# Router of a mixture-of-experts block: gathered rows made already turned, router tiles in groups of two, one and one, a fifth weight slot filled early, table work around the first SiLU product

## The reference

```
h = rmsnorm(x, ffn_norm)
g_logits = h @ w_group                       # 8 groups
g_sel = argmax(g_logits);  g_w = softmax(g_logits)[g_sel]
e_logits = (h @ w_expert)[group g_sel]       # 8 experts of a group
top_p, top_i = top_k(softmax(e_logits), 2)
gates = g_w * top_p / sum(top_p)
for each of the 2 choices e of a token:
    y += gate * ((silu(h @ w1[e]) * (h @ w3[e])) @ w2[e])
out = rmsnorm(x + y)
```

## Time and profile before

| | before |
|---|---|
| median of 3 runs | 1443.67 us (1443.07 to 1448.06) |
| profiled execution, device time | 1446.29 us |
| its span of instructions | 1444.5 us |
| PE busy | 1389.5 us, 96% |
| DVE busy | 528.9 us, 37% |
| ACT busy | 515.6 us, 36% |
| POOL busy | 473.9 us, 33% |
| read from HBM | 289.27 MB, 202 GB/s over the span |
| chain that ended last, by engine | PE 23%, DMA 13%, DVE 1% |

### The profile page before, as it was taken

One profiled execution on the slowest core, in us unless ns is written; L12 is line 12 of the kernel. 1 busy time (PEld: TensorE's weight loads), 2 busy tenths in 40 slices (PEclk: granted clock), 3 DMA queues, 4 the chain that ended last, 5 costly groups with the idle time before them and its releaser, 6 DMA issues. The chain is left out here.

```text
span 1444.5 us, 26677 instructions
## 1 busy us (share of the span) xinstructions
PE 1389.5 (96%) x11124; PEld 1041.7 (72%) x11124; DVE 528.9 (37%) x1262; ACT 515.6 (36%) x1084; POOL 473.9 (33%) x457
## 2 busy tenths in 40 slices
PE   8999999999999999999999999999999999988986
PEld 7788876677888888888767886876666665655553
DVE  3103217742221200221245404264554554454435
ACT  5325448863332222222346333232223222222222
POOL 5334646543544444444356844410000000000000
PEclk9999999999999999999999999999999999999998
DMA  5223225314133034131232311669999999999994
GB/s 188 83 94 117 97 82 159 105 36 140 59 117 117 30 109 150 62 117 68 82 117 73 117 59 59 241 266 378 411 419 419 420 418 419 421 419 420 420 419 195
DMA packets 89577, 293.22 MB, mean 203 GB/s; under 512 B 9324, under 2 KB 38160, under 8 KB 64880
## 3 DMA queue, kind: packets, MB, share of 16 engines
q1 hardware_dynamic: 89056, 290.35, 52.1%
q0 software_dynamic: 288, 1.05, 0.2%
q10 hardware_dynamic: 112, 0.09, 0.0%
HBM read 289.27 MB, written 2.13 MB: 202 GB/s over the span
## 5 line engine op out<-in xcount | busy, mean ns | idle before, releaser
L504 POOL TENSOR_TENSOR wring_halves<-wring,wring_halves 128x512 fp32r<-128x512 f32 x274 | 357.1, 1308 | 374.4 <-ACT wring_halves L499 372.8
L499 ACT CAST wring_halves<-wring 128x512 fp32r<-128x512 f32 x274 | 168.8, 621 | 450.4 <-PE ps L1239 426.7
L1237 PE MATMUL ps<-wring_halves,big_halves 128*128 128x512 f32 x612 | 241.9, 395 | 0.6 <-POOL wring_halves L504 0.5
L1237 PE MATMUL ps<-hT_halves,wring_halves 128*128 128x512 f32 x480 | 188.2, 392 | 2.4 <-DVE big_halves L2026 2.4
L1239 PE MATMUL ps<-hT_halves,wring_halves 128*128 128x512 f32 x480 | 187.5, 391 | 0.0
L1238 PE MATMUL ps<-big_halves,wring_halves 128*128 128x512 f32 x480 | 187.3, 390 | 0.0
L2721 POOL TENSOR_TENSOR rstd<-rstd,half 128x1 f32<-128x1 f32 (+1 forms) x21 | 12.1, 581 | 506.5 <-DVE rstd L2674 477.7
L1238 PE MATMUL ps<-wring_halves,hT_halves 128*128 128x512 f32 x436 | 170.9, 392 | 0.0
L1239 PE MATMUL ps<-wring_halves,hT_halves 128*128 128x512 f32 x436 | 170.7, 392 | 0.0
L1237 PEld LDWEIGHTS ps<-wring_halves,big_halves 128*128 128x128 f32 x612 | 115.7, 189 | 27.8 <-POOL wring_halves L504 2.7
L1788 PE MATMUL ps<-xn,fixed 128*128 128x512 f32 x256 | 120.0, 612 | 0.4 <-DVE fixed L2469 0.4
(11 more groups left out here) (354 smaller groups left out, 1984.3 us busy)
## 6 DMA issues: line engine op xcount, KB each, us to landing
big<-in_moe_w_dram SPq DMA_DIRECT2D x90, 1024.0 KB, 25.4
wring<-in_moe_w_dram SPq DMA_DIRECT2D x70, 1024.0 KB, 25.2
wring<-in_ffn_w_in_dram SPq DMA_DIRECT2D x22, 1024.0 KB, 7.2
hT<-in_moe_w_dram SPq DMA_DIRECT2D x20, 1024.0 KB, 25.8
wring<-in_fox_w_in_dram SPq DMA_DIRECT2D x7, 2048.0 KB, 8.7
wring<-in_gla_w_in_dram SPq DMA_DIRECT2D x6, 2048.0 KB, 8.4
mkv<-in_moe_w_dram SPq DMA_DIRECT2D x12, 1024.0 KB, 25.8
wring<-in_ffn_w_out_dram SPq DMA_DIRECT2D x4, 2048.0 KB, 7.9
```

Of the source, the lines that this page charges most:

```text
L499: act.copy(hi, src).then_inc(s_hi, 1)
L504: pool.tensor_tensor(lo, src, hi, ALU.subtract).then_inc(s_lo, 1)
L1237: pe.matmul(out, lhs[1], rhs[0], start=start, stop=False)
```

## The change

It has four parts.

- **Turned rows made directly.** For bunch 0, `turned_tokens(t, i)` takes the place of `tokens`, `tokens_out` and `xT`. The rows of `xn` are the stationary operand (128 columns with stride 8) and M is the moving one (128 columns), so the result is `xeT` as it is wanted: 32 products of 128x128 in two banks. The other bunches stay as they were; `s_G` and `s_Ge` count one bunch less.
- **Fifth down slot early.** `rtw` moves to the buffer `fixed`, `down_in(4, 4)` stands behind expert 1's pieces, and SP's wait for `s_lg` goes.
- **Table work around the first SiLU product.** Bunch 0's `placesT` goes behind expert 0's gate/up; six small operations (`spilled_places`) behind `hid(0)`, bunch 1's choices behind `hT_out(0)`, and the gates' arithmetic ahead of `hid(0)`.
- **Router in groups of two, one and one.** `picks`, `ranks` and `choices` take a list of tiles: (0, 1), (2), (3). The counts of all tokens get a bank of their own (`LOGIT_BANKS[2]`). `moe_row(3)` moves from ahead of tile 2's picks to behind its choices, and ScalarE copies the counts only after the last choice (`s_M`).

The core of the diff (SP, ACT, PE, DVE; index changes inside `picks` and `ranks` left out):

```diff
-        rtw = mkv[:, 0:KD * NR].rearrange("p (k n) -> p k n", k=KD)
+        rtw = fixed[:, 912:912 + KD * NR].rearrange("p (k n) -> p k n", k=KD)
...
                 down_in(e, e)
+            down_in(4, 4)
             sp.wait_ge(*tile_release["gwo0"])
...
             gate_up_in(5, 5)
-            sp.wait_ge(s_lg, T)
-            down_in(4, 4)
...
-            act.wait_ge(s_pre, 2)
-            act.copy(cnt, bank(LOGIT_BANKS[1])[:, 2 * EXPERTS:3 * EXPERTS]).then_inc(s_cntc, 1)
+            act.wait_ge(s_M, T)
+            act.copy(cnt, bank(LOGIT_BANKS[2])[:, EXPERTS:2 * EXPERTS]).then_inc(s_cntc, 1)
...
-            tokens_out(0, 0)
-            tokens_out(0, 1)
-            placesT_out(0, 0, 6)
-            xT_out(0, 0, 5)
-            xT_out(0, 1, 7)
+            xT_out(0, 0, 0)
+            xT_out(0, 1, 1)
...
                 silu(b, b)
+                if b == 0:
+                    placesT_out(0, 0, 6)
...
-            added_up(1, [(ones, again(0, 3), 0), (ones, again(1, 3), 0)])
+            added_up(1, [(ones, ohs[:, 0:1, :], 0), (ones, ohs[:, 1:2, :], 0)], True, False)
...
+            def turned_tokens(t, i):
+
+                pe.wait_ge(s_M, t + 1)
+                pe.wait_ge(s_hnrow, t + 1)
+                rows = xn[:, t, :].rearrange("p (m k) -> p k m", k=KD)
+                for k in range(4):
+                    last = pe.matmul(bank(i)[:, k * R:(k + 1) * R], rows[:, 4 * i + k, :], one_hots(0)[1][:, t, :],
+                                     start=(t == 0 and k == 0), stop=(t == T - 1), skip_group_check=True)
+                if t == T - 1:
+                    last.then_inc(s_xTp, 1)
...
-            pe.wait_ge(s_hnrow, T)
-            tokens(0, 0, range(0, 2))
             pe.wait_ge(s_oh, 2)
-            added_up(1, [(ones, again(2, 2), 1), (strict, ohs[:, 2:4, :], 0), (ones, ohs[:, 3:4, :], 2)]).then_inc(s_pre, 1)
-            tokens(0, 1, range(0, 2))
-            tokens(0, 0, range(2, 4))
-            tokens(0, 1, range(2, 4))
-            placesT(0, 6)
-            pe.wait_ge(s_cntc, 1)
-            xT(0, 0, 5)
-            xT(0, 1, 7)
+            added_up(1, [(strict, ohs[:, 2:3, :], 0)], False, True).then_inc(s_pre, 1)
+            added_up(2, [(ones, again(0, 2), 0), (ones, again(1, 2), 0), (ones, again(2, 2), 0)], True, False)
+            turned_tokens(0, 0)
+            turned_tokens(1, 0)
+            pe.wait_ge(s_oh, 3)
+            added_up(2, [(strict, ohs[:, 3:4, :], 0), (ones, ohs[:, 3:4, :], 1)], False, True).then_inc(s_pre, 1)
+            turned_tokens(0, 1)
+            turned_tokens(1, 1)
+            for t in (2, 3):
+                turned_tokens(t, 0)
+                turned_tokens(t, 1)
...
                 expert_in(b)
+                if b == 0:
+                    pe.wait_ge(s_cntc, 1)
+                    placesT(0, 6)
...
-            for p in range(2):
-                picks(p)
-                if p == 0:
-                    output_added(1, T - 1)
-                ranks(p)
-                if p == 0:
-                    moe_scale(T - 1)
-                choices(0, val, range(2 * p, 2 * p + 2))
-                if p == 0:
-                    dve.wait_ge(s_pw, roots.n)
-                    moe_row(T - 1)
+            picks((0, 1))
+            output_added(1, T - 1)
+            ranks((0, 1), 0, 1)
+            moe_scale(T - 1)
+            choices(0, val, (0, 1))
+            picks((2,))
+            dve.wait_ge(s_pw, ROOTS_AHEAD_OF_ROUTER)
+            picks((3,))
...
+            ranks((2,), 1, 2)
+            choices(0, val, (2,))
+            moe_row(T - 1)
+            ranks((3,), 2, 3)
+            choices(0, val, (3,))
...
                     hT_out(b, b)
+                    if b == 0:
+                        bunch_choices(1)
```

More of the change, by code:

```diff
@@ L532, in program @@
         LOGIT_BANKS = SUM_BANKS[1]
+        ROOTS_AHEAD_OF_ROUTER = 1 + 6 * T
         def row_part(v, t, i):
@@ L1757, in _, with added_up @@
             out_projection(first_pair)
-            def added_up(p, parts):
+            def added_up(p, parts, start, stop):
                 for i, (m, v, at) in enumerate(parts):
@@ L1763, in added_up @@
                     last = pe.matmul(bank(LOGIT_BANKS[p])[:, at * EXPERTS:(at + n) * EXPERTS].rearrange("p (t n) -> p t n", t=n), m[:, :], v,
-                                     start=(i == 0 and at == 0), stop=(i == len(parts) - 1), skip_group_check=True)
+                                     start=(start and i == 0), stop=(stop and i == len(parts) - 1), skip_group_check=True)
                 return last
@@ L2418, in _, with picks @@
             dve.wait_ge(s_cst, 2)
[L2420 to L2424, removed]
+            def picks(tiles):
+                a, n = tiles[0], len(tiles)
+                ts = slice(a, a + n)
+                for t in tiles:
                     dve.wait_ge(s_lg, t + 1)
@@ L2427, in picks @@
                 me.wait()
-                for t in (2 * p, 2 * p + 1):
+                for t in tiles:
                     me.inc(dve.max(gm8[:, t, :], lg[:, t, 0:GROUPS]))
                 me.wait()
-                for t in (2 * p, 2 * p + 1):
+                for t in tiles:
                     me.inc(dve.max_index(gi_u[:, t * 8:t * 8 + 8], gm8[:, t, :], lg[:, t, 0:GROUPS]))
@@ L2444, in picks @@
                 picked = ei_u[:, :].rearrange("p (t n) -> p n t", t=T)[:, 0:2, ts]
[L2445 to L2461, removed]
+                chosen = of_tiles(ohall, tiles)
@@ new lines, in picks, with of_tiles @@
+                me.link(dve.tensor_tensor(chosen, ioe.unsqueeze(1).unsqueeze(1).to_broadcast([P, 2, n, EXPERTS]),
+                                          picked.unsqueeze(3).to_broadcast([P, 2, n, EXPERTS]), ALU.is_equal))
+                dve.tensor_tensor(ohs[:, ts, :], chosen[:, 0, :, :], chosen[:, 1, :, :], ALU.add).then_inc(s_oh, 1)
+                me.inc(dve.tensor_copy(of_tiles(esel, tiles), picked))
+            def of_tiles(v, tiles):
+                p, i = divmod(tiles[0], 2)
+                four = v[:, 4 * p:4 * p + 4]
+                four = four.rearrange("p (k t) n -> p k t n", k=2) if len(v.shape) == 3 else four.rearrange("p (k t) -> p k t", k=2)
+                return four[:, :, i:i + len(tiles)]
@@ new lines, in ranks @@
+            def ranks(tiles, b, prefixes):
+                n = len(tiles)
+                r, q, w = of_tiles(rk, tiles), of_tiles(q1, tiles), of_tiles(val, tiles)
+                before = bank(LOGIT_BANKS[b])[:, 0:n * EXPERTS].rearrange("p (t n) -> p t n", t=n)
+                dve.wait_ge(s_pre, prefixes)
+                me.link(dve.tensor_tensor(of_tiles(ohp, tiles), of_tiles(ohall, tiles),
+                                          before.unsqueeze(1).to_broadcast([P, 2, n, EXPERTS]), ALU.mult))
+                me.link(dve.tensor_reduce(r, of_tiles(ohp, tiles), AX, ALU.add))
+                me.inc(dve.tensor_scalar(q, r, C - 0.5, 2.0 * C * EXPERTS, ALU.is_ge, ALU.mult))
+                me.link(dve.scalar_tensor_tensor(out=w, in0=of_tiles(esel, tiles), scalar=float(C), in1=r, op0=ALU.mult, op1=ALU.add))
+                me.link(dve.tensor_tensor(w, w, q, ALU.add))
@@ L2620, in _ @@
                         bunch_places(b - 1)
+                    if b == 0:
+                        spilled_places()
                     hT_out(b, b)
+                    if b == 0:
+                        bunch_choices(1)
                     if b == 3:
```

31 lines of the change are left out of this document (15 added, 16 removed).

## The result

| | before | changed |
|---|---|---|
| median of 22 runs each | 1443.91 us | 1447.76 us |
| lowest to highest | 1440.68 to 1448.36 | 1445.9 to 1452.12 |
| profiled execution, around its span | 1446.29 around 1444.5 | 1448.02 around 1446.2 |

The ratio is 1.0027, with a 95% interval of 1.002 to 1.0034: about 3.9 us slower, where 3.9 us faster was forecast and 1437.9 to 1443.9 given as the range.

The account below looks back on a forecast made before the run. The kernel was taken to end with the experts' weight stream plus a fixed tail. Expert 0's gate/up 3.9 us earlier and later holes 3.8 earlier gave -3.8 to -3.9, so 1439.8 us against 1443.67; range 1437.9 to 1443.9.

Parts of the forecast that it names:

- the price of one record of the new product: TensorE's 64 new gather records: 0.125 us each, taken from the prefix sums, between floor 0.109 and ceiling 0.147.
- the stride shows no price: TensorE's new stationary operand: reading with a stride of 8 elements was claimed to cost nothing extra.
- rows 6: Profile rows of G's strided loads in the turning passes: 128 loads, median 193 ns against a least of 185.
- ceiling of 0.147: Upper bound in us for one record of TensorE's new product, from six prefix-sum records in 0.88 us.
- slower rival: TensorE's 128-column stationary loads not hidden beside products: 0.213 us a record, time +1.5, 1445.2 us; chance 0.05.
- VectorE's chain: VectorE's router tables in the new order: last choice at 968.7 us, 0.8 later than before; gates done at 973.0.
- the clock rival: TensorE's clock falls again during tile 3 and expert 0: gain only 2.2, time 1441.4 us; chance 0.09.
- the second hole of the stream: Weight stream's shortfall in 1005 to 1020 us: 1.9 us missing before, still 1.5 to 2 expected around 1001 to 1016.
- the early slot alone: Fifth down piece sent early into the idle stretch before 940: nothing booked by itself, bounds 0 and 1.5 us.
- VectorE's ceiling: Rival: one tile costs VectorE as much as two, last choice at 971.9; gain 0.8, 1442.9 us; chance 0.10.
- TensorE's floor: Rival: 0.109 us a record and VectorE's half prices, gate/up ends 971.6; gain 5.2, 1438.5 us; chance 0.12.
- nothing arrives: Rival: last weight pieces held by slots, not the stream, so the time stays at 1443.7 us; chance 0.06.

Follow-up runs that it names:

- e2: Changed kernel with normalized rows written by k, VectorE writing with a step of 128 elements, so stationary blocks are contiguous: 1444.28 us, ratio 0.9996.
- e1: Changed kernel with bunch 0's products reading 128 neighbouring columns instead of every eighth (wrong columns, times only): 1440.34 us, ratio 0.9968.
- e10: Changed kernel with rows laid out by twos: VectorE writes in four instructions, TensorE reads with stride 2; whole result computed: 1441.01 us, ratio 0.9972.
- e7: Changed kernel with rows laid out by fours: VectorE in two instructions reading runs of four, TensorE reading with stride 4: 1447.14 us, ratio 1.0022.
- e9: Changed kernel with every fourth column of a stretch of 512 as stationary block (wrong columns): 1447.54 us in one execution.
- e5: Kernel before with only the router's weights in the other buffer and the fifth down piece sent early: 1444.61 us, ratio 1.0005.
- e13: e4 with the table work as before too, leaving the early slot and the router groups: 1443.03 us, ratio 0.9985.
- e12: e10 with the fifth down piece sent late as before, after all logits: 1443.68 us, ratio 0.9991.
- e8: Changed kernel with every second column of a stretch of 256 as stationary block (wrong columns): 1439.81 us in one execution.
- e11: e10 with tile 3's rows scaled by ScalarE and multiplied by the gains on GpSimd instead of VectorE: 1442.49 us, ratio 0.9982.
- e6: Changed kernel with rows kept by k, VectorE reading with a step of 8 and writing contiguously: 1444.03 us, ratio 1.0001.
- e4: Changed kernel with bunch 0 gathered as before (gather, copy, eight turning passes), the rest of the change kept: 1441.94 us, ratio 0.9983.

## Why the prediction was wrong

**The failed step** is the price of one record of the new product: "nearest by shape are the prefix sums ... so 0.125", with the sentence "the stride shows no price". Measured: 0.2375 to 0.242. 64 x 0.115 is 7.4 us; the forecast of -3.9 with 7.4 added is +3.5. In the frame of before, the products start at 962.26 (forecast 962.0) and end at 978.09 (forecast 970.75). In the frame of before the pair goes out at 977.41 + 2.77 = 980.2, 3.4 later than 976.79, and down 3's issue 3.55 later than 1005.51. Everything behind that step worked as described, with the sign turned.

**How rows 6 misled.** They compare turning passes with turning passes, all of them strided, by their own least value. The fair partner stood in the same trace, the turning of M, which is contiguous: 140 ns against 193 (lines 1812 and 1806 above; line 1803 of the kernel before has the same median of 140). In e2, where G is contiguous as well, line 1806 has a median of 140. So the stride cost 53 ns already, under work that hid it: eight turning passes in 1.13 us are 0.14 each. Nor would 53 have been the right surcharge, since the load of a product pays 144 (192 to 336). The unmeasured thing was the load of an FP32 product with a stride of 8, and its ceiling of 0.147 came from contiguous operands alone. A ceiling should have taken the strided load as one that no product hides.

**The slower rival had the right sign and the wrong mechanism.** It put a record at 0.213 and the time at 1445.2. (It calls 0.107 the spacing of the logits; the earlier trace rows give 0.109, so two of them are 0.219.) It decides "from 0.19 us a record on", and the records went past that. But loads of this shape do lie beside the products, 0.111 a record in e1; it is the strided load that can't be hidden. The rule cited there from the Trainium skill, "TensorE: Matmul & The Clock Gate", Part 3, is not borne out by e1. Another page speaks for the step between stride 2 and 4: the Trainium skill, "SBUF — State Buffer", says in "Specifications (TRN2)" that a 16-byte line of SBUF needs at least two hits for full bandwidth. A stride of 2 gives two FP32 elements a line, a stride of 4 one, and 196 and 330 ns agree. The turning passes don't: their loads have a median of 209 ns at a stride of 2 (line 1806 in e10) and 193 at 8. A note under "Door 1: The DMA port swizzle" on that page puts the free stride at 4 FP32 elements; here e7 and e9 contradict it, and the measurement decides.

**Right:** VectorE's chain (last choice forecast for 968.7, measured 966.07 + 2.77 = 968.8); the clock, 1.00 through 966 to 969, so that the clock rival falls; the end of the kernel following the first pair's issue; the second hole of the stream, 2.1 us for a forecast 1.5 to 2; the early slot alone at nothing (e5); the moved table work almost without effect (e13). VectorE's ceiling and TensorE's floor did not come up, and "nothing arrives" is refuted by e1, e7 and e10, which move the end both ways with the chain. The forecast from tile 3's logits to the end of expert 0's gate/up, 959.13 to 972.9, is 13.8 us; e1, with contiguous loads, has 13.84 to the issue behind it. Only half right was that the early slot is worth nothing: e12 says so no longer when the chain is faster. e10, whose records take 0.118 each, comes to the forecast gain, but that is partly luck: by the traces its pair goes out 3.3 us earlier behind the logits (14.32 for 17.66) and down 3's issue 3.1 (43.24 for 46.38), its dearer row scaling costs 0.4 ahead of the logits (14.39 for 13.96 from the first row scaling to tile 3's logits), and the slot that was booked at nothing makes up for it at least in part.

## What to carry to other kernels

Price a new operand by rows of the same mode and the same access pattern; where the trace has none, compare strided with contiguous rows of another mode to see whether a stride costs at all, and take the unhidden price as a bound. A layout that suits TensorE is paid for by the engine that writes it: look for one in which both find two neighbours, as pairs here. A part that is worth nothing beside a slow chain should be tried again once the chain is fast.

## What the runs showed of the hardware

- An FP32 weight load of 128x128 for a product takes 192 ns at stride 1 (e1), 196 at 2 (e8, e10), 330 at 4 (e7, e9) and 336 at 8 (the changed kernel). A record takes 0.111, 0.118, 0.233 and 0.24 us with them. The loads lie over each other, since each is longer than the spacing.
- A load for a turning pass has a median of 140 ns contiguous (e2), 209 at stride 2 (e10), 213 at 4 (e7) and 193 at 8, so pairs don't help there. These loads were hidden in this kernel.
- VectorE's scaling of 128x1024 with two inputs takes 1.28 us contiguous, 2.0 to 2.1 writing with a step of 128 elements, 2.1 to 2.2 reading with a step of 8, 1.42 in two instructions with runs of four, 1.67 in four instructions with pairs.
- Three VectorE operations grew by 0.5 to 0.7 us each while GpSimd multiplied, and others beside them did not (e11).
- The granted clock fell to 0.50 after TensorE had idled 1.86 us (before), 1.85 (e5), 1.54 (e2) and 2.10 (e6), and in e11 after 0.68. It stayed at 1.00 after 0.76 (e10), 0.88 (e4), 1.32 (e2) and 1.45 (e6). So the length of the idle time alone doesn't tell; why it fell in e11 was not tested.
